# Loading the narrow weights first, and writing the position table to DRAM straight from eight SBUF partitions

## The reference, cut to what matters

```python
def _mixer_ab(x, w_in, w_gate, b_gate, g_norm, w_out, rel_table):
    y = x @ w_in
    qa, ka, va, ra, ga, qb, kb, vb, qi, ki, wi = _split(y, AB_SPLITS)
    g_log = jax.nn.log_sigmoid((ga @ w_gate + b_gate)) / GLA_GATE_TAU
    oa = _gla(qa, ka, va, g_log)                       # gated linear attention
    oa = rms(oa) * g_norm * jax.nn.silu(ra)
    ob = _dsa(qb, kb, vb, qi, ki, wi, rel_table)       # indexer, top-64 keys, attention
    return jnp.concatenate([oa, ob], axis=-1) @ w_out

# in _dsa:  score = sum_h wi[t, h] * relu(qi[t, h] . ki[s]);  keep the 64 best keys
#           logits = qb . kb / 8 + rel_table[bucket(t - s)];  softmax;  times vb
```

## Time and profile before

| what | value |
|---|---|
| profiled execution, whole time | 1984.51 us |
| its span in the profile | 1982.4 us |
| median of three runs | 1986.87 us |
| PE busy | 1868.7 us (94%) |
| DVE busy | 1374.0 us (69%) |
| ACT busy | 1110.4 us (56%) |
| POOL busy | 50.5 us (3%) |
| chain that ended last: PE | 87% |
| chain that ended last: DMA | 1% |

### The profile page before, as it was taken

One profiled execution on the slowest core, in us unless ns is written; L12 is line 12 of the kernel. 1 busy time (PEld: TensorE's weight loads), 2 busy tenths in 40 slices (PEclk: granted clock), 3 DMA queues, 4 the chain that ended last, 5 costly groups with the idle time before them and its releaser, 6 DMA issues.

```text
span 1982.4 us, 26182 instructions
## 1 busy us (share of the span) xinstructions
PE 1868.7 (94%) x10221; PEld 1589.4 (80%) x10221; DVE 1374.0 (69%) x1207; ACT 1110.4 (56%) x1031; POOL 50.5 (3%) x49
## 2 busy tenths in 40 slices
PE   6999899989979999999999999999999978779998
PEld 5897799968967878878888788787887858669997
DVE  3642544453468888888788888888988875955544
ACT  4532344434536767777776777776767743334343
POOL 0000100010020000000000000000000000010000
PEclk9997899988979999999999999999999988789999
DMA  9631455542357989999999899998999972314551
GB/s 283 223 128 56 159 189 190 184 137 83 128 171 273 372 312 366 343 328 369 333 345 370 308 367 344 334 372 307 365 342 333 366 264 83 120 64 164 186 190 43
DMA packets 252154, 490.43 MB, mean 247 GB/s; under 512 B 14178, under 2 KB 96651, under 8 KB 251716
## 3 DMA queue, kind: packets, MB, share of 16 engines
q1 hardware_dynamic: 248144, 474.74, 68.5%
q0 software_dynamic: 3184, 14.29, 2.2%
q10 hardware_dynamic: 772, 0.65, 0.1%
HBM read 488.56 MB, written 5.80 MB: 249 GB/s over the span
## 4 chain that ended last, share of the span: by engine, by line
PE 87%; DVE 8%; issue 2%; ACT 2%; DMA 1%; POOLq 0%; SPq 0%; DVEq 0%; POOL 0%; ACTq 0%
PE psum L525 26%; PE psum L527 25%; PE psum L528 25%; DVE ta L1940 2%; PE psum L966 2%; PE psum L1038 2%; PE psum L1012 1%; DVE wl L1501 1%; PE psum L586 1%; PE psum L671 1%; PE psum L613 1%; PE psum L645 1%; PE psum L618 1%; DVE u L1884 1%; PE psum L698 1%
## 5 line engine op out<-in xcount | busy, mean ns | idle before, releaser
L1501 DVE TENSOR_TENSOR wl<-ring,wh 128x2048 fp32r<-128x2048 f32 x446 | 1021.9, 2291 | 401.7 <-ACT wh L1131 401.2
L1131 ACT ACTIVATE wh<-ring 128x2048 fp32r<-128x2048 f32 x450 | 861.5, 1915 | 424.8 <-PE psum L525 354.7
L525 PE MATMUL psum<-wh,xTh 128*128 128x512 f32 (+1 forms) x1168 | 448.0, 384 | 7.1 <-DVE wl L1501 3.0
L527 PE MATMUL psum<-wl,xTh 128*128 128x512 f32 (+1 forms) x1168 | 438.0, 375 | 0.0
L528 PE MATMUL psum<-wh,xTl 128*128 128x512 f32 (+1 forms) x1168 | 437.8, 375 | 0.0
L525 PE MATMUL psum<-xTh,wh 128*128 128x256 f32 x1088 | 314.7, 289 | 13.9 <-DVE wl L1501 11.3
L527 PE MATMUL psum<-xTl,wh 128*128 128x256 f32 x1088 | 312.2, 287 | 0.0
L528 PE MATMUL psum<-xTh,wl 128*128 128x256 f32 x1088 | 311.9, 287 | 0.0
L525 PEld LDWEIGHTS psum<-wh,xTh 128*128 128x128 f32 x1168 | 221.8, 190 | 49.2 <-issue 10.8
L528 PEld LDWEIGHTS psum<-wh,xTl 128*128 128x128 f32 x1168 | 221.2, 189 | 41.0
L527 PEld LDWEIGHTS psum<-wl,xTh 128*128 128x128 f32 x1168 | 221.7, 190 | 39.9 <-issue 1.9
(11 more groups left out here) (260 smaller groups left out, 1215.4 us busy)
## 6 DMA issues: line engine op xcount, KB each, us to landing
ring<-in_w_moe SPq DMA_DIRECT2D x336, 1024.0 KB, 5.2
ring<-in_w_dense SPq DMA_DIRECT2D x33, 1024.0 KB, 5.2
ring<-in_w_in_ab SPq DMA_DIRECT2D x14, 1024.0 KB, 11.3
ring<-in_w_in_cd SPq DMA_DIRECT2D x12, 1024.0 KB, 5.3
ring<-in_w_gate SPq DMA_DIRECT2D x11, 1024.0 KB, 5.3
ring<-in_w_up SPq DMA_DIRECT2D x11, 1024.0 KB, 5.3
ring<-in_w_down SPq DMA_DIRECT2D x11, 1024.0 KB, 4.9
ring<-in_w_in SPq DMA_DIRECT2D x10, 1024.0 KB, 6.0
```

Source lines behind the costliest of these rows:

```text
L525: last = pe.matmul(o, a[0], b_[0], start=first, stop=False)
L527: pe.matmul(o, a[0], b_[1], start=False, stop=False)
L1131: act.activation(upper_half[i], ring[:, u_, :], ACT.Copy).then_inc(hi_ready[s_], 1)
L1501: dve.tensor_tensor(lower_half[i], ring[:, u_, :], upper_half[i].bitcast(F32), ALU.subtract)\
```

## The change

It has two parts.

**The order at the start.** SP issues the six narrow loads ahead of units 0 and 1. ACT, DVE and PE follow: ACT splits the narrow weights and issues its eleven loads of constants before it splits units 0 and 1; PE multiplies `ki` and the narrow columns first and the two units after them.

**The position tables.** The 8 x 384 pieces no longer pass through `rel_rows` in DRAM. POOL writes each table's 128 copies to `rel_scratch` directly from the eight SBUF partitions, with a source view that repeats each row 128 times; the outermost dimension of both sides is the eight heads. `rel_out` now counts these large writes, and `bias_table` has no wait of its own.

```diff
-            load_all([cols(win[0], c) for c in AB_ORDER[:2]])
             for part, c, src in ((early, 0, win[0][:, :, AB["ga"]:AB["ga"] + 16]),
...
-            load_all([cols(win[0], c) for c in AB_ORDER[2:]])
+            load_all([cols(win[0], c) for c in AB_ORDER])
...
@@ tensor
             transposes(x, 0)
-            proj_transposed()
-            proj_transposed()
             pe.wait_ge(narrow_lo, 1)
...
             narrow(early, 0, 24)
+            proj_transposed()
+            proj_transposed()
             pe.wait_ge(consts_in, CONSTS)
@@ scalar
             copy_transposed()
-            upper()
-            upper()
             act.wait_ge(small_in, 96)
             act.activation(wnh[:, :], wnraw, ACT.Copy).then_inc(narrow_hi, 1)
...
-            copy_step(ta[:, 0:2, :])
             upper()
-            copy_step(ta[:, 2:4, :])
             upper()
             act.activation(kiT[:, :], step_out()[:, 0:T], ACT.Copy).then_inc(step_evac, 1)
...
+            copy_step(ta[:, 0:2, :])
+            upper()
+            copy_step(ta[:, 2:4, :])
+            upper()
             log_sigmoid_parts(step_out()..., gz[:, :, :], ga_[:, :, :])
@@ vector
             lower_transposed()
-            for _ in range(2):
-                lower()
             dve.wait_ge(narrow_hi, 1)
             dve.tensor_tensor(wnl[:, :], wnraw, wnh[:, :].bitcast(F32), ALU.subtract).then_inc(narrow_lo, 1)
-            for _ in range(2):
+            for _ in range(4):
                 lower()
@@ gpsimd
             def bias_table(i):
-                pool.wait_ge(rel_spread[i], 16)
...
             for i in range(3):
                 pool.wait_ge(step_evac, 7 + i)
-                pool.dma_start(rel_rows[i], relrow[:, i, :]).then_inc(rel_out, 16)
+                pool.dma_start(rel_dram[i].rearrange("t h j -> h t j"),
+                               relrow[:, i, :].unsqueeze(1).broadcast_to([H, P, REL])).then_inc(rel_out, 16)
             pool.wait_ge(rel_out, 48)
-            for i in range(3):
-                pool.dma_start(rel_dram[i], rel_rows[i].unsqueeze(0).broadcast_to([P, H, REL])).then_inc(rel_spread[i], 16)
             bias_table(0)
             pool.wait_ge(filled, 3)
             rstd_of(8)
```

## The result

The changed kernel takes 2017.13 us (median of four runs, 2014.10 to 2018.16) against 1988.15 for the kernel before on the same chip: a ratio of 1.0146, 95% interval 1.0128 to 1.0165, 29 us slower. The forecast was 2001 with a range of 1985 to 2026: the direction held and the time is inside the range, but the loss is twice the 14.3 us of the sum. The profiled execution took 2011.46 us, its span is 2009.7 against 1982.4, so the trace has 27.3 us to explain.

A forecast was written before the change was run, and what follows sets the result against it. PE was taken to bound the kernel, ending 87% of the wait chain. The start's 0.5 us gain brought the copies' issue to 42.8; late tables then cost PE 14.3 us: 1986.87 + 14.3 = 2001 us, range 1985 to 2026.

The forecast's parts named there:

- the sum: Tables land at 137.2, DVE goes on at 139.8, PE waits before unit 12: +14.3 us, 2001 us against the median.
- the step that failed: PE before unit 12: undelayed until 130.0, then waits until 144.8 instead of starting at 130.52, +14.3 us.
- The start: New load order on SP, ACT and PE: gates start at 35.8 instead of 36.78; net gain 0.5 us.
- the gates' copy: Gates' first copy on ACT falls behind unit 3's split, 2.5 us behind the gates instead of 2.0: 0.5 us given back.
- The tables' duration: Three big copies out of eight partitions: 91.1 us at two engines' worth, plus 3.3 fixed; ends 18.8 and 230.
- The rule of the Trainium skill: Partitions 0 to 3 share one SBUF port, 4 to 7 another; at 27.2 GB/s each, copies take 86.7 us, time 1996.8.
- The other rule: Copies run on the largest engine count up to 16 dividing both outermost dimensions, here eight: 22.8 us, nothing late.
- The weights have cover: Weight units during the table copies: unit 10 asked for at 62.79, used up before 120.77; units 2 to 9 already in SBUF.
- Rival 3: Weights starve beside table rows: 30.4 us a unit, unit 12 split near 144; hardly adds, counted within the forecast's range.
- rival 1: At POOL's wait ahead of the power: tables take at most 76.3 us, so stay hidden; 1986.4 us, chance 0.29.
- rival 2: Table copies run at one engine's worth or less: 182 us, PE +105, 2092 us; chance 0.09.
- The signs I had asked for: Tables landing 80 to 110 us after issue, POOL's wait ending near 137, long DVE wait, one 14 us PE gap, gates near 36.

## Where the prediction held, and the step that failed

*The start.* Forecast: a gain of 0.5 us, between 2 gained and 4 lost. Alone it measured as no change. Its steps were off by more than their sum: the narrow loads had landed at 14.53 and not 13.2, unit 1 at 23.98 and not 21.3, and PE waited 1.75 us for a small copy behind unit 1's split on ACT, where I had it done by 24.0. What I said of the gates' copy, that it comes to stand behind a split, happened and cost 1.3 us (3.7 in the whole change). None of it decided anything.

*The tables' duration.* Two engines' worth and 3.3 us were 94.4 us; measured 97.5, from 47.00 to 144.53. The landing came 7.3 us behind my 137.2, of which 4.2 are the later start. The size of this term held, but by luck more than by reasoning: the rows bounded it at 18.8 and 230 us, nothing in them singled out two engines' worth, and the copies ran on eight engines each, not on two. The rule of the Trainium skill that spoke against the part ("SBUF — State Buffer", "Door 1: The DMA port swizzle") gives the reason, and the traces agree: 28, 52 and 100 us for partitions four apart, two apart and side by side, which is eight, four and two ports by its map. By its 27.2 GB/s a port the copies would have taken 86.7 us; less the fixed 3.3 us they took 94, which is 25 GB/s a port, and the measurement decides. The other rule ("DMA: Bandwidth & Descriptors", "Why a DMA increments its semaphore by 16 and not by 1") agrees as well, but not as I had used it. A copy with eight as its outermost dimension does run on eight engines, as the share of 0.49 shows; that says how many engines it holds, not how fast they get on.

*The step that failed* is the sum's last one: "PE, which has the first scores behind it, stands before unit 12 from 130.0 until 144.8 instead of starting it at 130.52: +14.3 us." The sum takes PE as undelayed until 130, on the strength of "The weights have cover" and of nothing at all about instructions. In its place the trace has two fetch gaps of 9.32 and 9.43 us with their restarts, 21.8 us of delay, a late unit 11, and POOL done 4.69 us before DVE asks. The weights' cover held for unit 10 and failed for unit 11, and the instructions had cover for 14 us of lateness where 23 to 25 came. Where the premise is made true, with one copy at a time, the step measures right: from a landing of 150.60, 13.4 us behind mine, it gives 14.3 + 13.4 = 27.7 us; PE's gap is 26.3 and the ratio says 25.4. That the whole time, 2017, still lay inside the range of 1985 to 2026 is no merit of the mechanism: the range was wide because of the copies' duration, which was not what was off.

*Rival 3* had the mechanism in hand, that "every engine alternates between a table row and a weight row", and priced it at nothing, since it looked only at the units that PE would need near 140. Its 30.4 us a unit was too kind: unit 11 took 69.1 us to land. And it did not ask who else is served by these engines. The hidden case (rival 1) and one engine's worth (rival 2) are excluded by the 97.5 us.

*The signs I had asked for:* the tables landed 94 us behind their issue, as said; POOL's wait ended at 144 and not 137; DVE's wait before L1755 was not long but 1.9 us; the gates started at 39.89 and not near 36; "the long gap of PE stands elsewhere" was on my list of what would show the forecast wrong, and that is what came.

## What to carry to other kernels

Before a DMA goes out of a few neighbouring SBUF partitions, count two things: the ports behind them, which set its rate here, and the engines that it holds with long packets, which decide who suffers. Spread the rows over the partitions (four apart here). Keeping slow copies on some of the engines took away the gaps here, but not the lateness. And ask of any slow DMA not just who waits for it, but what else those engines carry in that time, PE's instructions included. A wait labelled "issue" in the middle of a run of matmuls, beside a DMA share near 1 at a small GB/s, is how the late fetch looks in a profile; a long wait for a split whose weights are late is how the other half looks, and in the run with three extra copies it was the larger one.

## What the runs showed of the hardware

- Instruction fetches suffer from packets of other DMAs. With all 16 held by packets of 1.36 us a fetch came 23 to 25 us later than before (77.15 and 81.11 against 53.6 to 56.54), and PE stood still for 9 to 11 us; what it had in hand lasted until 73.98, 17 us past the time at which the fetch used to come. With eight engines held by one copy at a time, the same two fetches came at 53.5 and 68.3 to 68.5, on time, but two later ones, during the second copy, 13.1 and 9.7 us behind PE's progress. Which engines serve a fetch, and why it comes so many packets late, the records don't say.
- PE fetched 16384 bytes at a time, 256 of its instructions, and stopped when the fetch for the next 256 had not come: behind its records 705, 961 and 1217. 256 instructions lasted it about 16 us in this stretch.
- 4608-byte packets out of partitions 0 to 7 took 0.70 us with one copy under way and 1.36 us with two or more, at the same 50 GB/s. Out of partitions 0, 4, ..., 28 they took 0.33 us at some 190 GB/s. So the source partitions were the limit, and a second copy at the same time bought nothing but longer packets.
- Cutting a slow transfer into two DMAs that run at once made the kernel about 9 us slower (ratios of 1.0002 and 1.0047 to the kernel before) with no byte more.
